# Routed-expert stage of a two-layer decoder step: gather in float32r parts, packed token slots, turned router product, extra-item table beside item 0

## The chip, the cores and the metric

The kernel runs on one core of a Trainium2 chip, as one program. The metric is the device time of an execution in microseconds (us). A core has five engines with instruction streams of their own: PE (TensorE, the 128x128 matrix array; its weight loads are shown apart as PEld), DVE (VectorE), ACT (ScalarE), POOL (GpSimd) and SP (SyncE, which only issues DMA here). They wait for each other through semaphores. SBUF is the on-chip memory of 128 partitions; PSUM has eight banks of 128 x 512 fp32, into which PE writes. TensorE's clock is granted at one of two levels, 2.4 GHz (1.00 in the profile) and 1.2 GHz (0.50).

## The reference

One inference step of two layers over 288 tokens (256 of a prompt, 8 x 4 of samples), 1024 features. Each layer has a mixer of four head groups with a projection, a residual and a LayerNorm, then a feed-forward part, again with residual and LayerNorm. Layer 0's feed-forward part is a dense SwiGLU. Layer 1's is the one that the change touches:

```python
logits = (h @ w_router).astype(jnp.float32)          # 8 experts
top_logit, top_e = lax.top_k(logits, TOP_K)          # the best two for each token
gates = jax.nn.softmax(top_logit, axis=-1)
...
def expert_block(args):                              # a block of up to 128 tokens of one expert
    tok, e = args
    xb = h_pad[tok]
    return (jax.nn.silu(xb @ w_gate[e]) * (xb @ w_up[e])) @ w_down[e]
...
f = zeros.at[sorted_tok].add(y_assign * w_assign[:, None])
h = layer_norm(ALPHA * h + f, ln_ffn_g, ln_ffn_b)
```

The hidden width is 3584. All values are fp32, and the result must be that of fp32 products.

## The kernel before

Everything is laid out with features in partitions: `h` and `r` are 8 blocks (KB) of 128 features x 288 tokens. The two layers run one after the other. All weights come as a stream of 1 MB chunks (128 x 2048 fp32) through a ring of six slots (`ring`), in the order in which they are used; SP issues the load of a chunk when the chunk six places earlier has been cut (`lo_done`).

*Cutting.* A product of fp32 values is made as three products of the type float32r (fp32r), which is of less precision: each operand is split into a high part, rounded to fp32r by an ACT copy, and a low part, which DVE gets by subtracting the high part. hi x hi, hi x lo and lo x hi are summed in PSUM. So each weight chunk costs ACT one copy (`w_hi`, L883 in the expert part) and DVE one subtraction (`w_lo`, L1253). `w_hi` and `w_lo` have three places each (SPLIT), and a chunk can be cut when PE is done with the chunk three places earlier (`chunk_done`).

*Routing* (ahead of the experts). When the LayerNorm `mix1` has given all eight blocks of h, PE multiplies them by `w_router` (L581): weights are the tokens of h, moving are the 8 columns of the router, 3 tiles of tokens (128, 128, 32) x 8 blocks, in plain fp32. Then it transposes h into token rows (L589, 24 transposes); DVE and ACT copy these from PSUM to `h_tok`. DVE meanwhile finds the best two experts for each token in small steps, each of which waits for the one before it (`step`, semaphore `route`). PE counts the tokens of each expert in order (L596, L599), DVE makes of it each token's slot in each expert (`item_pos`) and its gate (`item_gate`), and `select` makes the 0/1 matrix `sel` of the first expert (tokens x 128 slots). Then follows the table of extra items: an expert with more than 128 tokens needs further items, and a list of them is worked out in some thirty small steps on 128 partitions (L1189 to L1216). It ends in `table`, whose first entry is the number of items; with these inputs it is 8, one for each expert. PE, ACT and DVE read it (`value_load`) before their loop over the items. Last come eight multiplications `r = ALPHA * h` (L1219).

*An item* is one expert with up to 128 token slots. PE gathers its tokens in two halves of four blocks (`gather`, L608): in each block the three token tiles of `h_tok` are the weights and `sel` is moving, 12 fp32 products of 128 columns for each half, into bank 2 or 3. ACT and DVE cut the result to `x_hi` and `x_lo`, columns 0 to 127 of each block of 288. Then PE does, in seven groups of 512 hidden columns, the gate and the up products (24 fp32r products of 512 columns each, L617, with x as weights and the weight chunk moving), a transpose of the activated values (L647) and the down products (24 as well, with `ad_hi` and `ad_lo` as weights). There are 42 chunks for each item (CPI). ACT does silu and the cuts, DVE the multiplication with up, the low parts and the cuts. The gather of the next item's first half stands behind the last transpose, ahead of the last down products, and that of its second half behind them; then PE spreads the item's output back to the tokens with the transposed `sel` (`scat`): 8 blocks of two products (L701, L702), each added to `r` by DVE (L1275, semaphore `added`). The output parts `y_hi` and `y_lo` lie in columns 128 to 255 of x_hi's and x_lo's blocks; DVE makes y_lo at L1267. The last item gathers once more, for nobody.

*The end.* When all additions are done, PE sums `r` for the last LayerNorm (`ffn1`; L410 the mean, L415 the squares), DVE and ACT finish it, and SP stores h in two halves.

The order on each engine is that of the program text; no scheduler changes it. The engine functions share only semaphores, so a step that is moved on one engine moves past the waits that stand there.

## Time and profile before

| | |
|---|---|
| time, median of 3 runs | 1707.34 us (1707.08 to 1708.59) |
| span of the profiled execution | 1707.8 us |
| PE / PEld / DVE / ACT / POOL busy | 94% / 81% / 73% / 57% / 8% |
| DMA | 428.63 MB, mean 251 GB/s |
| expert part, from the first gather to the end | 613.8 to 1707.8 us |

The page cuts the span in 40 slices. PE is at 9 tenths in nearly all of the expert part, and the granted clock is full there but for the first slice or so (PEclk). A matmul's duration in the trace is longer than the distance to the next one, since they are pipelined: what one costs is the distance of starts. One fp32 product is two records of the trace (and two weight loads), one fp32r product is one record. A wait that is put down to a semaphore names the instruction that came last.

### The profile page before, as it was taken

To read this page: it belongs to the slowest core of one execution; us is meant where nothing else is said; L and a number is where in the kernel's file an instruction comes from. 1 tells how busy PE (TensorE), PEld (TensorE's weight loads), DVE (VectorE), ACT (ScalarE), POOL (GpSimd) and SP (SyncE) were. 2 spreads that over 40 slices of the span, in tenths; PEclk is the share of its full clock that TensorE was granted. 3 is DMA by queue.
4 is the path that set the end of the run, shared out by engine and by line. 5 is a ranking of instruction groups with operands and counts; after the bars stand their busy time and mean duration, and the time that the engine had idled before them with its cause. 6 is when DMAs were issued, how large, how long until landed. Compare 5 with 4: busy or idle time off the path is not lost.

```text
span 1707.8 us, 22408 instructions
## 1 busy us (share of the span) xinstructions
PE 1604.5 (94%) x8460; PEld 1380.0 (81%) x8460; DVE 1245.5 (73%) x1176; ACT 966.8 (57%) x816; POOL 140.0 (8%) x128
## 2 busy tenths in 40 slices
PE   4868999989886799999999999999999999999996
PEld 3857999989785788888888888888888888888885
DVE  3894443444679458878878878888888888887883
ACT  4333333334433327767767767767767767776772
POOL 3545000000055200000000000000000000000000
PEclk8979999999998969999999999999999999999998
DMA  9328355445333609989988998998997997997980
GB/s 282 129 94 115 107 172 173 150 147 173 124 99 99 89 27 355 359 293 348 359 325 316 359 345 304 362 333 305 361 360 277 361 376 264 369 367 262 371 300 28
DMA packets 213985, 428.63 MB, mean 251 GB/s; under 512 B 9136, under 2 KB 66416, under 8 KB 213936
## 3 DMA queue, kind: packets, MB, share of 16 engines
q1 hardware_dynamic: 209024, 424.67, 70.1%
q0 software_dynamic: 1984, 2.10, 2.1%
q10 hardware_dynamic: 2928, 1.18, 0.3%
q8 instruction: 33, 0.54, 0.1%
q14 instruction: 16, 0.13, 0.0%
HBM read 425.55 MB, written 2.37 MB: 251 GB/s over the span
## 4 chain that ended last, share of the span: by engine, by line
issue 66%; PE 24%; DVE 7%; ACT 1%; DMA 1%; POOL 0%; SPq 0%; ACTq 0%; DVEq 0%; POOLq 0%
PE bank L437 21%; DVE work L1014 4%; DVE w_lo L917 2%; DMA ring<-in_w_in 1%; PE bank L410 1%; ACT h L806 0%; ACT w_hi L744 0%; PE bank L415 0%; PE bank L503 0%; PE bank L424 0%; DVE r L910 0%; POOL rstd_tok L1289 0%; DVE r L944 0%; DVE work L1010 0%; DVE h L944 0%
## 5 line engine op out<-in xcount | busy, mean ns | idle before, releaser
L1253 DVE TENSOR_TENSOR w_lo<-ring,w_hi 128x2048 fp32r<-128x2048 f32 x320 | 732.3, 2290 | 120.0 <-ACT w_hi L883 119.1
L883 ACT ACTIVATE w_hi<-ring 128x2048 fp32r<-128x2048 f32 x320 | 614.1, 1919 | 181.3 <-PE bank L617 181.2
L617 PE MATMUL bank<-w_hi,x_hi 128*128 128x512 f32 x896 | 360.4, 402 | 0.3
L617 PE MATMUL bank<-w_hi,x_lo 128*128 128x512 f32 x896 | 354.1, 395 | 0.0
L617 PE MATMUL bank<-w_lo,x_hi 128*128 128x512 f32 x896 | 353.3, 394 | 0.0
L437 PE MATMUL bank<-x_hi,w_hi 128*128 128x288 f32 x832 | 255.1, 307 | 13.2 <-DVE x_lo L923 10.7
L437 PE MATMUL bank<-x_lo,w_hi 128*128 128x288 f32 x832 | 250.8, 301 | 0.0
L437 PE MATMUL bank<-x_hi,w_lo 128*128 128x288 f32 x832 | 249.8, 300 | 0.0
L617 PEld LDWEIGHTS bank<-w_hi,x_lo 128*128 128x128 f32 x896 | 168.8, 188 | 40.0
L617 PEld LDWEIGHTS bank<-w_hi,x_hi 128*128 128x128 f32 x896 | 169.0, 189 | 38.2 <-issue 2.1
L617 PEld LDWEIGHTS bank<-w_lo,x_hi 128*128 128x128 f32 x896 | 169.6, 189 | 37.0
L744 ACT ACTIVATE w_hi<-ring 128x2048 fp32r<-128x2048 f32 x68 | 129.4, 1908 | 108.6 <-PE bank L437 106.4
L617 PE MATMUL bank<-w_hi,ad_hi 128*128 128x512 f32 x448 | 175.7, 392 | 0.0
L917 DVE TENSOR_TENSOR w_lo<-ring,w_hi 128x2048 fp32r<-128x2048 f32 x60 | 139.8, 2330 | 48.6 <-ACT w_hi L744 48.3
L617 PE MATMUL bank<-w_lo,ad_hi 128*128 128x512 f32 x448 | 175.0, 391 | 0.0
L617 PE MATMUL bank<-w_hi,ad_lo 128*128 128x512 f32 x448 | 174.4, 389 | 0.0
L437 PEld LDWEIGHTS bank<-x_hi,w_hi 128*128 128x128 f32 x832 | 161.7, 194 | 15.0 <-issue 10.9
L437 PEld LDWEIGHTS bank<-x_lo,w_hi 128*128 128x128 f32 x832 | 161.8, 194 | 0.6
L437 PEld LDWEIGHTS bank<-x_hi,w_lo 128*128 128x128 f32 x832 | 161.9, 195 | 0.0
L1289 POOL TENSOR_TENSOR rstd_tok<-var_tok,minus_half 128x3 f32<-128x3 f32 x9 | 9.2, 1020 | 1490.2 <-DVE var_tok L936 1490.2
L617 PEld LDWEIGHTS bank<-w_hi,ad_hi 128*128 128x128 f32 x448 | 84.1, 188 | 19.3
L617 PEld LDWEIGHTS bank<-w_hi,ad_lo 128*128 128x128 f32 x448 | 84.1, 188 | 18.0
(194 smaller groups left out, 1670.8 us busy)
## 6 DMA issues: line engine op xcount, KB each, us to landing
ring<-in_w_e_gate SPq DMA_DIRECT2D x112, 1024.0 KB, 5.6
ring<-in_w_e_up SPq DMA_DIRECT2D x112, 1024.0 KB, 5.4
ring<-in_w_e_down SPq DMA_DIRECT2D x112, 1024.0 KB, 5.5
ring<-in_w_in SPq DMA_DIRECT2D x16, 1024.0 KB, 9.2
ring<-in_w_ff_gate SPq DMA_DIRECT2D x14, 1024.0 KB, 5.0
ring<-in_w_ff_up SPq DMA_DIRECT2D x14, 1024.0 KB, 5.1
ring<-in_w_ff_down SPq DMA_DIRECT2D x14, 1024.0 KB, 4.9
ring<-in_w_out SPq DMA_DIRECT2D x8, 1024.0 KB, 5.5
```

The costliest lines, as they stand in the source:

```text
L410: last = mm(bank[6][:, 0:TOKENS], weights[:, :], x[:, b, :], start=(b == 0), stop=(b == nb - 1))
L437: ins = mm(out, w, x, start=(first and n == 0), stop=(last and n == 2), skip_group_check=True)
L617: ins = mm(out, x, w[slot][:, columns], start=(first and n == 0), stop=(last and n == 2), skip_group_check=True)
L744: A(w_hi[c % SPLIT][:, :], ring[c % SLOTS][:, :], ACT.Copy).then_inc(hi_done, 1)
L883: A(w_hi[(START + p) % SPLIT][:, :], ring[(START + p) % SLOTS][:, :], ACT.Copy).then_inc(hi_done, 1)
L917: V.tensor_tensor(w_lo[c % SPLIT][:, :], ring[c % SLOTS][:, :], w_hi[c % SPLIT][:, :].bitcast(F32), ALU.subtract).then_inc(lo_done, 1)
L1014: V.scalar_tensor_tensor(out=out, in0=src, scalar=w, in1=out, op0=ALU.mult, op1=ALU.add).then_inc(conv_a, 1)
L1253: V.tensor_tensor(w_lo[(START + p) % SPLIT][:, :], ring[(START + p) % SLOTS][:, :], w_hi[(START + p) % SPLIT][:, :].bitcast(F32), ALU.subt ...
L1289: G.tensor_tensor(rstd_tok[:, :], var_tok[:, :], minus_half[:, :], ALU.pow).then_inc(ln_rs, 1)
```

## The change

Five edits:

1. The gather is made of fp32r products. `h_tok` becomes `h_tok_hi` and `h_tok_lo` (ACT copies, DVE subtracts, six pieces each in the order TURNS), `sel` is fp32r itself (0 and 1 are exact), and each of the 12 fp32 products becomes two fp32r products. All token tiles are taken with 128 rows; POOL writes zeros in the third tile first (`pad_ready`).
2. The token slots lie packed: `xs_hi`, `xs_lo`, `y_hi` and `y_lo` are views of x_hi and x_lo with 128 columns for each block, one behind the other, where they were columns of blocks of 288.
3. The router's logits come in the other orientation: the 8 columns of w_router are the weights and h moves (288 columns), one product for each block of h as soon as it is there, followed by the two transposes of this block's full token tiles. DVE copies the 8 x 288 logits (`logit_t`), and PE transposes them (three small transposes). The logits wait no more for st_v and for all of ln_out.
4. The table of extra items and `r = ALPHA * h` leave the way to item 0. They are a generator (`extra_items`), of which DVE runs two steps behind each cut of item 0. The number of items is therefore read only ahead of item 7: PE and ACT loop over items 0 to 6 and then from 7, DVE has item 0 written out, then 1 to 6, then from 7. In items up to 6 the cuts for the next item need no condition.
5. The last LayerNorm sums into bank 0 in place of 6 and waits for each block's addition by itself; the output is stored in four pieces in place of two.

```diff
-        h_tok, at = part(work, at, TT, D_MODEL)
         gate_e, at = part(work, at, 2, GC)
-        sel, at = part(work, at, TT, W)
         sel_w, at = part(work, at, TT, W)
+
+        def over_work(name, shape):
+
+            nonlocal at
+            t = nc.alloc_sbuf_tensor_at(name, shape, F32R, offset=work_at + 4 * at)
+            at += int(np.prod(shape[1:]))
+            assert at <= FB * TOKENS
+            return t
+
+        h_tok_hi = over_work("h_tok_hi", [P, TT, D_MODEL])
+        h_tok_lo = over_work("h_tok_lo", [P, TT, D_MODEL])
+        sel = over_work("sel", [P, TT, W])
         at = 0
 
-        y_hi, y_lo = x_hi[:, :, W:2 * W], x_lo[:, :, W:2 * W]
+        def slots_of(x, n):
+            flat = x[:, :, :].rearrange("p k t -> p (k t)")
+            return flat[:, n * KB * W:(n + 1) * KB * W].rearrange("p (k n) -> p k n", k=KB)
+
+        xs_hi, xs_lo = slots_of(x_hi, 0), slots_of(x_lo, 0)
...
+        y_hi, y_lo = slots_of(x_hi, 1), slots_of(x_lo, 1)
...
+        MEAN_BANK = {n: 0 if n == "ffn1" else 6 for n in LNS}
+        TURNS = [(0, 0), (1, 0), (0, 1), (1, 1), (2, 0), (2, 1)]
...
+            for q in range(4):
+                sp.wait_ge(ln_out, LN_AT["ffn1"] + 2 * (q + 1))
+                sp.dma_start(y_out[:, 2 * q:2 * q + 2, :], h[:, 2 * q:2 * q + 2, :]).then_inc(st_y, 16)
+            sp.wait_ge(st_y, 64)
...
-            pe.wait_ge(ln_out, LN_AT["mix1"] + KB)
+            def turn_tokens(t, k):
+                rows = TILE_ROWS[t]
+                return nc.tensor.transpose(bank[2 + 2 * t + k // 4][0:rows, k % 4 * P:(k % 4 + 1) * P],
+                                           h[:, k, t * P:t * P + rows], ident)
+
+            for k in range(KB):
+                pe.wait_ge(ln_out, LN_AT["mix1"] + k + 1)
+                last = mm(bank[0][0:N_EXPERTS, 0:TOKENS], w_router[:, k, :], h[:, k, :], start=(k == 0),
+                          stop=(k == KB - 1))
+                if k == KB - 1:
+                    last.then_inc(logits_ready, 1)
+                for t in range(2):
+                    last = turn_tokens(t, k)
+                    if k % 4 == 3:
+                        last.then_inc(h_turned, 1)
+            for half in range(2):
+                for k in range(4 * half, 4 * half + 4):
+                    last = turn_tokens(2, k)
+                last.then_inc(h_turned, 1)
+            pe.wait_ge(logits_out, 1)
             for t in range(TT):
                 rows = TILE_ROWS[t]
-                for k in range(KB):
-                    last = mm(bank[0][0:rows, t * 8:t * 8 + 8], h[:, k, t * P:t * P + rows], w_router[:, k, :],
-                              start=(k == 0), stop=(k == KB - 1))
-            last.then_inc(logits_ready, 1)
-
-            for t in range(TT):
-                rows = TILE_ROWS[t]
-                for half in range(2):
-                    for k in range(4):
-                        last = nc.tensor.transpose(bank[2 + 2 * t + half][0:rows, k * P:(k + 1) * P],
-                                                   h[:, 4 * half + k, t * P:t * P + rows], ident)
-                    last.then_inc(h_turned, 1)
+                last = nc.tensor.transpose(bank[1][0:rows, 64 + t * 8:64 + t * 8 + 8], logit_t[0:8, t * P:t * P + rows],
+                                           ident[0:8, 0:8])
+            last.then_inc(logits_turned, 1)
...
-                        rows = TILE_ROWS[t]
-                        last = mm(bank[2 + half][:, k % 4 * W:(k % 4 + 1) * W],
-                                  h_tok[0:rows, t, k * P:(k + 1) * P], sel[0:rows, t, :],
-                                  start=(t == 0), stop=(t == TT - 1))
+                        for rows in (h_tok_hi, h_tok_lo):
+                            last = mm(bank[2 + half][:, k % 4 * W:(k % 4 + 1) * W],
+                                      rows[:, t, k * P:(k + 1) * P], sel[:, t, :],
+                                      start=(t == 0 and rows is h_tok_hi), stop=(t == TT - 1 and rows is h_tok_lo))
...
+            pe.wait_ge(pad_ready, 3)
+            pe.wait_ge(h_tok_lo_done, 6)
             gather(0, 0)
             gather(0, 1)
             pe.sem_inc(chunk_done, SPLIT)
-            pe.wait_ge(table_ready, 1)
-            n_items = pe.value_load(table[0:1, 0:1], min_val=N_EXPERTS, max_val=N_EXPERTS + MAX_EXTRA)
-            with pe.Fori(0, n_items) as i:
+            pe.sem_inc(added, KB)
+
+            def item(i):
...
-            pe.wait_ge(added, n_items * KB + KB)
-            large_ln("ffn1", lambda b: None)
+
+            with pe.Fori(0, N_EXPERTS - 1) as i:
+                item(i)
+            pe.wait_ge(table_ready, 1)
+            n_items = pe.value_load(table[0:1, 0:1], min_val=N_EXPERTS, max_val=N_EXPERTS + MAX_EXTRA)
+            with pe.Fori(N_EXPERTS - 1, n_items) as i:
+                item(i)
+            large_ln("ffn1", lambda b: pe.wait_ge(added, n_items * KB + b + 1))
...
-            for t in range(TT):
+            for n, (t, half) in enumerate(TURNS):
                 rows = TILE_ROWS[t]
-                act.wait_ge(h_turned, 2 * t + 2)
-                A(h_tok[0:rows, t, 512:1024], bank[3 + 2 * t][0:rows, :], ACT.Copy).then_inc(h_tok_act, 1)
+                if n == 4:
+                    act.wait_ge(pad_ready, 3)
+                act.wait_ge(h_turned, n + 1)
+                A(h_tok_hi[0:rows, t, half * 512:(half + 1) * 512], bank[2 + 2 * t + half][0:rows, :],
+                  ACT.Copy).then_inc(h_tok_hi_done, 1)
...
-            dve.wait_ge(ln_out, LN_AT["mix1"] + KB)
-            dve.wait_ge(st_v, 128)
             step(V.memset(logit[:, :, :], 0.0))
             dve.wait_ge(logits_ready, 1)
-            V.tensor_copy(logit[:, 0:2, :], bank[0][:, 0:16].rearrange("p (t e) -> p t e", t=2))
-            V.tensor_copy(logit[0:N_SAMPLE, 2, :], bank[0][0:N_SAMPLE, 16:24]).then_inc(route, 1)
+            V.tensor_copy(logit_t[0:N_EXPERTS, :], bank[0][0:N_EXPERTS, 0:TOKENS]).then_inc(logits_out, 1)
+            dve.wait_ge(logits_turned, 1)
+            V.tensor_copy(logit[:, 0:2, :], bank[1][:, 64:80].rearrange("p (t e) -> p t e", t=2))
+            V.tensor_copy(logit[0:N_SAMPLE, 2, :], bank[1][0:N_SAMPLE, 80:88]).then_inc(route, 1)
...
-            for t in range(TT):
-                dve.wait_ge(h_turned, 2 * t + 1)
-                rows = TILE_ROWS[t]
-                V.tensor_copy(h_tok[0:rows, t, 0:512], bank[2 + 2 * t][0:rows, :]).then_inc(h_tok_dve, 1)
+            dve.wait_ge(pad_ready, 3)
+            for n, (t, half) in enumerate(TURNS):
+                dve.wait_ge(h_tok_hi_done, n + 1)
+                rows, at = TILE_ROWS[t], slice(half * 512, (half + 1) * 512)
+                V.tensor_tensor(h_tok_lo[0:rows, t, at], bank[2 + 2 * t + half][0:rows, :],
+                                h_tok_hi[0:rows, t, at].bitcast(F32), ALU.subtract).then_inc(h_tok_lo_done, 1)
...
+            def extra_items():
+
+                for d in range(KB):
+                    V.tensor_scalar(r[:, d, :], h[:, d, :], ALPHA, None, ALU.mult).then_inc(r_start, 1)
+                    yield
...
+                        next(beside, None)
...
+            beside = extra_items()
+            item(0, beside=beside)
+            for _ in beside:
+                pass
+            with dve.Fori(1, N_EXPERTS - 1) as i:
+                item(i)
+            dve.wait_ge(table_ready, 1)
+            n_items = dve.value_load(table[0:1, 0:1], min_val=N_EXPERTS, max_val=N_EXPERTS + MAX_EXTRA)
+            with dve.Fori(N_EXPERTS - 1, n_items) as i:
+                item(i, n_items)
...
+                if layer + 1 == DEPTH:
+                    pool.wait_ge(st_v, 64 * DEPTH)
+                    pool.wait_ge(ln_xn, LN_AT["mix1"] + KB)
+                    for v in (h_tok_hi, h_tok_lo, sel):
+                        G.memset(v[:, 2, :].bitcast(F32), 0.0).then_inc(pad_ready, 1)
```

On PE, between the LayerNorm mix1 and the first item. Before (L581 router, L589 transposes of h with the identity in `cst`, L596 and L599 counts, L608 the two gathers of item 0, all of `work`, where h_tok and sel lie):

```order
L424 MATMUL bank<-cst,rstd_tok 128x32
L581 MATMUL bank<-w_router,h 128x8 x16
L581 MATMUL bank<-w_router,h 32x8 x8
L589 MATMUL bank<-cst,h 128x128 x16
L589 MATMUL bank<-cst,h 32x128 x8
L596 MATMUL bank<-ybuf,cst 128x8
...
L599 MATMUL bank<-ybuf,ones 128x8 x3
L608 MATMUL bank<-work 128x128 x24
L627 TENSOR_LOAD table
```

and now (L607 router, L602 transposes of h, L622 transposes of the logits, L641 gather):

```order
L447 MATMUL bank<-cst,rstd_tok 128x32
L607 MATMUL bank<-h,w_router 8x288
L602 MATMUL bank<-cst,h 128x128 x2
...
L602 MATMUL bank<-cst,h 32x128 x8
L622 MATMUL bank<-cst,ybuf 128x8 x2
L622 MATMUL bank<-cst,ybuf 32x8
L629 MATMUL bank<-ybuf,cst 128x8
...
L641 MATMUL bank<-sel,h_tok_hi 128x128
L641 MATMUL bank<-sel,h_tok_lo 128x128
```

The router's products and the transposes take turns, block by block (eight such pairs), ahead of the third tile's transposes; the read of the table has left this place, and a gather has 24 products in place of 12.

On DVE, from the first selection to the cuts of item 0. Before (L1171 the selection, L1186 the counts, L1189 to L1216 the table, L1219 r, L1225 x_lo of item 0, L1234 sel_w, L1253 the first cut):

```order
L1171 TENSOR_SCALAR work<-cst,ybuf 32x128
...
L1186 COPY ybuf<-bank 128x8
L1189 TENSOR_SCALAR ybuf<-ybuf 128x8
...
L1216 CAST table<-ybuf 1x5
L1219 TENSOR_SCALAR r<-h 128x288 x8
L1225 TENSOR_TENSOR x_lo<-bank,x_hi 128x4x128 x2
L1230 TENSOR_LOAD table
...
L1253 TENSOR_TENSOR w_lo<-ring,w_hi 128x2048
```

and now (L1230 the selection, L1245 the counts, L1297 x_lo, L1306 sel_w, L1325 the cuts, L1250 r, L1254 and on the table, L1315 the multiplication with up):

```order
L1230 TENSOR_SCALAR sel<-cst,ybuf 32x128
...
L1245 COPY ybuf<-bank 128x8
L1297 TENSOR_TENSOR x_lo<-bank,x_hi 128x512 x2
...
L1325 TENSOR_TENSOR w_lo<-ring,w_hi 128x2048
L1250 TENSOR_SCALAR r<-h 128x288 x2
...
L1315 TENSOR_TENSOR work<-work,bank 128x512
L1325 TENSOR_TENSOR w_lo<-ring,w_hi 128x2048
L1254 TENSOR_SCALAR ybuf<-ybuf 128x8
```

The table's 29 instructions and the eight of r stand behind the first 17 cuts of item 0 now, where they stood ahead of x_lo.

## Rows read from the trace of the kernel before

The rows stand in groups, in the order in which the prediction comes to them. In rows of parts 5 of the page and of the groups of instructions the columns are: line, engine, operation, output<-inputs, shapes, count, then busy us and mean ns of one, then the idle time ahead of them and what ended it.

**Rows 1.** Part 1 of the page: busy us, share of the span, instructions.

```profile
PE 1604.5 (94%) x8460; PEld 1380.0 (81%) x8460; DVE 1245.5 (73%) x1176; ACT 966.8 (57%) x816; POOL 140.0 (8%) x128
```

**Rows 2.** Busy time by stage, one item: us, each engine's, clock, DMA, GB/s.

```profile
760.45:892.30 131.85, 131.72 (x607) 107.40 (x607) 110.81 (x74) 92.36 (x65) 0.00 (x0) 1.00 0.92 334
```

**Rows 3.** Parts 5 and 6 of the page: DVE's cuts; the weight loads.

```profile
L1253 DVE TENSOR_TENSOR w_lo<-ring,w_hi 128x2048 fp32r<-128x2048 f32 x320 | 732.3, 2290 | 120.0 <-ACT w_hi L883 119.1
...
ring<-in_w_e_down SPq DMA_DIRECT2D x112, 1024.0 KB, 5.5
```

**Rows 4.** Waits of SyncE's queue: us in total, times, longest.

```profile
SPq L382 <- DVE w_lo L1253: 815.9, 314, 55.0
```

**Rows 5.** Timeline, item 0 to item 1: start us, us, engine, line, operation, count.

```profile
746.64 4.19 PE L608 MATMUL bank<-work 128*128 128x128 f32 x24
...
750.76 0.19 PEld L617 LDWEIGHTS bank<-w_hi,ad_hi 128*128 128x128 f32 x1
750.87 0.19 PEld L617 LDWEIGHTS bank<-w_lo,ad_hi 128*128 128x128 f32 x1
751.10 0.39 PE L617 MATMUL bank<-w_lo,ad_hi 128*128 128x512 f32 x1
751.33 0.40 PE L617 MATMUL bank<-w_hi,ad_lo 128*128 128x512 f32 x1
...
756.34 4.18 PE L608 MATMUL bank<-work 128*128 128x128 f32 x24
757.98 1.40 DVE L1267 SCALAR_TENSOR_TENSOR x_lo<-bank,ybuf,x_hi 128x512 fp32r<-128x512 f32 x2
760.45 0.40 PE L701 MATMUL bank<-scat,x_hi 128*128 128x288 f32 x1
```

**Rows 6.** Timeline of PE in narrow windows: in the gather; one-column fp32 products.

```profile
746.98 0.69 PE L608 MATMUL bank<-work 128*128 128x128 f32 x3
...
747.18 0.79 PE L608 MATMUL bank<-work 32*128 32x128 f32 x3
...
769.12 0.38 PE L675 MATMUL bank<-ones,work 128*128 128x1 f32 x2
...
769.12 0.49 PE L675 MATMUL bank<-ones,work 128*128 128x1 f32 x3
```

**Rows 7.** Timeline, start of the expert part.

```profile
592.89 4.25 ACT L806 ACTIVATE h<-r,vec 128x288 f32<-128x288 f32 x8 [4.88 <-DVE r L944]
597.19 7.95 PE L581 MATMUL bank<-w_router,h 128*128 128x8 f32 x48 [4.83 <-ACT h L806]
...
605.07 5.38 PE L589 MATMUL bank<-cst,h 128*128 128x128 f32 x24
...
612.62 0.18 DVE L1163 SCALAR_TENSOR_TENSOR ybuf<-bank,ybuf 128x24 f32<-128x24 f32 x1 [2.23 <-issue]
...
621.60 1.82 DVE L1219 TENSOR_SCALAR r<-h 128x288 f32<-128x288 f32 x8
```

**Rows 8.** Busy time by stage, start of the expert part.

```profile
597.00:605.00 8.00, 7.81 (x48) 7.79 (x48) 0.08 (x1) 0.14 (x1) 0.00 (x0) 0.50 0.00 0
613.80:628.60 14.80, 14.74 (x48) 11.20 (x48) 9.09 (x44) 0.60 (x1) 0.00 (x0) 0.51 0.00 0
628.60:634.50 5.90, 5.90 (x15) 4.62 (x15) 3.08 (x5) 4.15 (x4) 0.00 (x0) 0.50 0.00 0
```

**Rows 9.** Groups of instructions: DVE on a 128x512 piece.

```profile
L1225 DVE TENSOR_TENSOR x_lo<-bank,x_hi 128x512 fp32r<-128x512 f32 x18 | 12.4, 691 | 44.3 <-ACT x_hi L857 44.3
```

**Rows 10.** One line, L617: duration ns min/median/max.

```profile
L617 PE MATMUL bank<-w_hi,x_lo x896: 387/396/628, 629.6 to 1661.6; 128*128 128x512 f32 x180
...
L617 PE MATMUL bank<-w_hi,ad_lo x448: 387/389/398, 656.0 to 1677.2; 128*128 128x512 f32 x150
```

**Rows 11.** Timeline of PE at the last LayerNorm.

```profile
1685.95 5.78 PE L410 MATMUL bank<-r,ones_model 128*128 128x288 f32 x16 [2.00 <-DVE r L1275]
```

**Rows 12.** Busy time by stage, the same stretch.

```profile
1685.90:1689.30 3.40, 3.35 (x7) 2.50 (x8) 0.00 (x0) 0.00 (x0) 0.00 (x0) 0.50 0.00 0
```

134 lines of the change are left out of this document (78 added, 56 removed).

## The prediction

> **What bounds the kernel now.** I read the page first, then the busy time by stage, the end of an item and the start of the next one instruction by instruction, and last the start of the expert part and the end of the kernel. The page says PE 94% busy, DVE 73%, ACT 57% [rows 1]; the chain of waits names no cause within the expert part, so it is of no use there. The stage table is: one item lasts 131.85 us, in which PE is busy for 131.72, DVE for 110.8 and ACT for 92.4 [rows 2]. TensorE bounds an item, and what it need not do comes off the time as long as nobody else gets late. The transfers do not yet: they land 5.5 us after their issue [rows 3], and SyncE spends 815.9 us waiting until DVE frees a slot of the ring [rows 4]. Around the last products of an item stand two gathers: from 746.64 to 750.76 (4.12 us) and from 756.34 to 760.45 (4.11 us) [rows 5]. Each is 12 fp32 products, which the trace shows as 24 records. So 8.23 us of each 131.85 are gathers.
>
> **The price of a gather, before.** The first four records, of two full tiles, start 0.113 us apart (746.64 to 746.98); then the 32-row tile begins 0.20 later [rows 5, 6]. Six records at 0.11 would be 0.67 us, while a group of three products takes 4.12/4 = 1.03: a third of the gather is the change of row size. After the change all three tiles have 128 rows, so this part goes. The Trainium skill (TensorEngine Tiling, Key Properties) says that a change of tiling mode drains the engine; the trace agrees, with about 0.09 us at that change. The rule speaks against the new router, which goes from 128 to 8 weight columns and back for each block.
>
> **The price of a gather, after.** It has 24 fp32r products with 128 moving columns. No row shows that shape. fp32r products with 512 columns start 0.23 us apart (751.10, 751.33) [rows 5]; in proportion 128 columns would take 0.057, the low end. But each product needs new weights. The first two fp32r loads after a gather are 0.11 apart (750.76, 750.87) [rows 5], and fp32 products with a single moving column take 0.11 more for one more [rows 6]: a load of 128 columns costs 0.11 whatever streams. The high end: fp32r gains nothing when few columns stream, and costs what the fp32 product of this very shape costs, two records, 0.22. I take 0.11, since the loads show it. A gather is then 24 x 0.11 = 2.64 us, the two 5.28 instead of 8.23: 2.95 less for each item. Eight items (the last one gathers too): -23.6. By the low end a gather is 1.37, another 20 off; by the high end 5.28, which is 1.17 more than now, and 16 of them +18.7 in place of -23.6.
> The Trainium skill (TensorE: Matmul & The Clock Gate, LDWEIGHTS) gives 128/1.2 = 107 ns for such a load, and the 0.11 confirms it. The same page (Weight-path perf modes) has a fast weight load for 128 columns of any type but FP32; by that rule fp32r would be near the low end. The two loads 0.11 apart do not show it.
>
> **Does anyone get late in an item?** After the second stretch of products the scatter needs y_lo, which DVE makes from 757.98 to 759.38, while the scatter starts at 760.45 [rows 5]. The first gather's end, and with it all of this, comes 1.48 earlier: y_lo from 756.5, its first half at 757.2, its second at 757.9. The scatter wants to start at 760.45 - 2.95 = 757.5; its first four blocks need the first half only. It just fits. DVE has 110.8 us of work in an item of then 128.9, so it stays below PE. Six chunks of 12 products at 0.23 take PE 16.6 us, three times the 5.5 of a landing, so the ring of six slots holds.
>
> **The start of the expert part.** ACT writes the eight h from 592.89 to 597.14; only then does the router start and take 7.95 us, and 24 transposes 5.38; DVE goes on with the counts at 612.62 and begins r at 621.60 [rows 7]. The gathers fill 613.8 to 628.6; the clock is half (1.2 GHz) then, in the router and until 634.5 [rows 8].
> - The router and the transposes now start with the first h, at 593.5. Eight router products of 288 columns are 16 records like those of L410: 5.78 us with 3.4 of them at half clock, so 4.1 at full [rows 11, 12] and 8.2 at half. With 24 transposes at 0.22 and 16 changes of columns at 0.09 that is 14.9 at half clock, 7.5 at full. If the clock rises some 6 us after the work starts, as it did in item 0 (628.6 to 634.5 [rows 8]), 60% are left for full clock: 4.5 more, so 604, and the three transposes of the logits 0.5 later, against 605.1 for the logits before: -0.6. Bounds: -3 at full clock, +4 at half.
> - DVE now has six subtractions of 0.69, as L1225 [rows 9], where it had three copies: at least three pieces more, +2. But before it stood idle for 2.23 us ahead of 612.62 [rows 7], because PE's counting stood behind the transposes; that wait goes. Both together: nothing. The first selection comes 0.6 earlier.
> - The 48 gather products: 0.22 each at half clock for 6 us (27 of them), then 21 at 0.11: 8.3 us against 14.8, -6.5 (-4.3 if the clock stays low). And item 0 starts at full clock: 5.9 us of half clock become 2.95: -3.
> - Sum of the start: -10 (from -4 to -13).
> - The table of extra items is 29 of the 41 small steps between 612.62 and 621.60, 0.22 each, so 6.4 us, and r 1.82 us [rows 7]: all of it lay beside the gathers. Now it stands between the cuts of item 0, two steps behind each of 17 cuts: 8.2 us more for DVE. Six chunks take PE 16.6 and four transposes, about 17.1; DVE needs 6 x 2.29 [rows 3] and two pieces of 0.69, 15.1, and with 12 steps 17.8 to 18. One microsecond late a group over three groups, less a lead of about one and a half: +1.5 (0 to 5).
> - The table is long ready when item 7 reads it. The read and the further copies of the loop I cost at nothing, since only one item boundary has them and PE is fed ahead there; +1 if not.
>
> **The end.** PE waited 2.00 us for the last addition, and L410 then ran at a clock of 0.50 for 3.4 us: 5.78 us, to 1691.73 [rows 11, 12]. Now each block's sum follows its addition, in a bank that the scatter does not use at that moment. From 1683.95 at full clock it ends at 1688.0: -3.7 (-2 if the clock drops all the same). The last output piece is half as big, 0.3 MB less at some 334 GB/s [rows 2]: -0.8. Sum -4.5.
>
> **Packing.** Gate and up products, whose weights are x_hi and x_lo at a step of 288, have a median of 396 ns; down products, whose weights lie packed at 128, 389 [rows 10]. If the step were the cause, the packed slots would give up to 6 ns x 2688 products = 16 us. The two kinds also differ in the banks they write and in how often they change them, and no row tells these apart. I put packing at nothing, and keep the 16 for the range.
>
> **The sum.** -23.6 - 10 + 1.5 - 4.5 = -36.6 from the span of the profiled execution, 1707.8, is 1671.2. The page gives no time around the span; the median of the runs, 1707.34, lies 0.5 below it. So 1670.7, rounded to 1670.
>
> **Rivals.**
> - Slower: fp32r with 128 moving columns takes as long as fp32 does. Its place is every gather, its price 24 x 0.22 = 5.28 against 4.11, +18.7 over 16 gathers; of the start's gain -4 is left, the end stays at -4.5, item 0 at +1.5: 1707.8 + 11.7, less 0.5, is 1719. A gather gets slower from 0.171 a product on (4.11/24), the kernel from about 0.19. For it: this kernel uses fp32r with 288 columns or more alone. Against it: the loads.
> - The change doesn't do what it says: the code turns fp32r of this width into the two records of fp32. The time is the same 1719.
> - Packing works (-16): 1655. For it the two medians, against it nothing but the other differences.
> - The low end, loads hidden (-20): 1651.
> - The boundary gives back half: once the gathers shrink, y_lo, x_lo and the additions on DVE are the chain, and PE waits 1.5 us an item, +12: 1682. For it: the margin above is 0.3 us. Against: DVE has 18 us an item to spare.
>
> **Chances and range.** Forecast 0.51 (1664 to 1676), half given back 0.11, packing 0.13, low end 0.05, fp32's price for fp32r 0.18 (both ways to it), gains and losses that cancel 0.02. 1650 to 1696 holds the first four and leaves the rest out. A measurement can tell 0.2%, 3.4 us, from no change: faster 0.80, same 0.02, slower 0.18.
>
> **What would show it.** In the gather 24 records, 0.11 apart at full clock and without a gap of 0.2; an item of 128.9 us; the first sum of the last norm beginning before the last addition ends; in item 0 a DVE without idle and PE waiting 1 to 2 us for w_lo. I am wrong if the fp32r records stand 0.2 apart, if gate and up products drop to 389 ns, or if PE waits for y_lo ahead of the scatter.

## The result, and the profile after

The kernel after takes 1662.66 us (median of 4 runs, 1661.68 to 1666.74), the kernel before 1707.62 us (4 runs, 1707.08 to 1708.59). The ratio is 0.9739 with a 95% interval of 0.9728 to 0.9751: faster by 45 us, where 1670 us in a range from 1650 to 1696 was forecast. The time lies inside the range, but below the band from 1664 to 1676 to which the forecast gave its chance of 0.51.

The profiled execution of after is its slowest run, 1666.74 us with a span of 1665.0. Both kernels run the same code up to the last LayerNorm ahead of the router, yet its first sum starts at 584.77 us here and at 580.44 in before. In the other kernels of this study it starts between 580.7 and 587.3, so the stretch ahead of it differs by up to 6.8 us from one execution to the next. It is left out of every comparison below; times are measured from that first sum on. From it to the end of the span before takes 1127.4 us and after 1080.2, 47.1 less.

Part 1 of the page, after, against [rows 1] (busy us, share of the span, instructions):

```profile
PE 1563.0 (94%) x8431; PEld 1362.1 (82%) x8431; DVE 1246.0 (75%) x1180; ACT 964.7 (58%) x817; POOL 141.8 (9%) x131
```

PE has 41.5 us less, DVE and ACT what they had: nobody else's work shrank, and TensorE still bounds the kernel. Next the boundary of items 0 and 1 in the timeline of after, against [rows 5] (start us, us, engine, line, operation, count), with records of the second gather picked out:

```profile
751.31 0.22 PE L641 MATMUL bank<-sel,h_tok_hi 128*128 128x128 f32 x1
751.37 0.28 PE L641 MATMUL bank<-sel,h_tok_lo 128*128 128x128 f32 x1
751.48 0.27 PE L641 MATMUL bank<-sel,h_tok_hi 128*128 128x128 f32 x1
751.59 0.28 PE L641 MATMUL bank<-sel,h_tok_lo 128*128 128x128 f32 x1
751.71 0.28 PE L641 MATMUL bank<-sel,h_tok_hi 128*128 128x128 f32 x1
...
752.95 1.41 DVE L1344 SCALAR_TENSOR_TENSOR x_lo<-bank,ybuf,x_hi 128x512 fp32r<-128x512 f32 x2
753.94 0.35 PE L735 MATMUL bank<-scat,x_hi 128*128 128x288 f32 x1
```

The 24 records stand 0.11 apart (0.06 between the first two) and without the gap of 0.2 at the change of row size. The gather takes 753.94 - 751.31 = 2.63 us (2.71 for the other one), where it took 4.11. y_lo, the low part of the item's output (L1344), begins 0.99 ahead of the scatter and its first half is done when the scatter starts: it just fits. The stage table of one whole item, after, against [rows 2]:

```profile
753.94:880.90 126.96, 126.90 (x607) 106.05 (x607) 110.76 (x75) 92.23 (x64) 0.00 (x0) 1.00 0.95 347
```

An item went from 131.6 (mean of the seven steps from scatter to scatter, 760.45 to 1681.55) to 127.06, so by 4.5 where the gathers explain 2.9. The rest is in the gate and up products. One line, L650, after, against [rows 10] (duration ns min/median/max):

```profile
L650 PE MATMUL bank<-w_hi,x_lo x896: 387/389/628, 627.4 to 1626.5; 128*128 128x512 f32 x180
```

Their median is 389 now, where it was 396; the down products had 389 all along. Last the end of the kernel, after, against [rows 11]:

```profile
1644.78 3.00 DVE L1353 TENSOR_TENSOR r<-r,bank 128x288 f32<-128x288 f32 x8
...
1645.65 4.09 PE L432 MATMUL bank<-r,ones_model 128*128 128x288 f32 x16
...
1659.28 3.48 SPq L419 DMA_DIRECT2D out_y_t<-h  x4
```

The mean sums start while DVE is still adding (L1353 ends at 1647.78), wait for nothing and take 4.09 us at full clock instead of 5.78.

All of it together, in us, from the two profiled executions:

| stretch | before | after | difference |
|---|---|---|---|
| up to the last norm ahead of the router (same code) | 580.44 | 584.77 | +4.3 |
| from there to the first gather product | 33.42 | 31.42 | -2.0 |
| the 48 gather products of item 0 | 14.76 | 10.27 | -4.5 |
| first product of item 0 to its scatter | 131.83 | 127.48 | -4.3 |
| first to eighth scatter (7 items) | 921.10 | 889.40 | -31.7 |
| eighth scatter to the end | 26.24 | 21.65 | -4.6 |

### The profile page after: what moved, and what is told of

It is laid out like the page before. It is cut to its first block, busy times and chain, and to the rows that moved or that the text cites. A ratio compares the mean times of both kernels' runs of the same rounds, so it can differ in the third digit from the quotient of the medians.

```text
span 1665.0 us, 22278 instructions
## 1 busy us (share of the span) xinstructions
PE 1563.0 (94%) x8431; PEld 1362.1 (82%) x8431; DVE 1246.0 (75%) x1180; ACT 964.7 (58%) x817; POOL 141.8 (9%) x131
## 4 chain that ended last, share of the span: by engine, by line
issue 65%; PE 23%; DVE 7%; DMA 3%; POOL 1%; ACT 1%; SPq 0%; ACTq 0%; POOLq 0%; DVEq 0%
PE bank L460 21%; DVE work L1071 4%; DVE w_lo L974 2%; DMA out_conv_c_s<-ext_c 1%; DMA ring<-in_w_in 1%; PE bank L432 1%; DVE r L1001 1%; PE bank L438 0%; PE bank L447 0%; PE bank L526 0%; POOL rstd_tok L1378 0%; ACT w_hi L784 0%; ACT h L846 0%; DVE r L966 0%; POOL ext_a L1396 0%
## 5 line engine op out<-in xcount | busy, mean ns | idle before, releaser
L1325 DVE TENSOR_TENSOR w_lo<-ring,w_hi 128x2048 fp32r<-128x2048 f32 x320 | 731.9, 2290 | 101.7 <-ACT w_hi L925 100.7
L650 PE MATMUL bank<-w_hi,x_hi 128*128 128x512 f32 x896 | 356.1, 397 | 1.4 <-issue 0.9
L650 PE MATMUL bank<-w_hi,x_lo 128*128 128x512 f32 x896 | 349.9, 390 | 0.0
L650 PE MATMUL bank<-w_lo,x_hi 128*128 128x512 f32 x896 | 349.2, 390 | 0.0
L650 PEld LDWEIGHTS bank<-w_hi,x_hi 128*128 128x128 f32 x896 | 168.7, 188 | 36.9 <-issue 2.7
L650 PEld LDWEIGHTS bank<-w_hi,x_lo 128*128 128x128 f32 x896 | 168.5, 188 | 36.1
L650 PEld LDWEIGHTS bank<-w_lo,x_hi 128*128 128x128 f32 x896 | 168.9, 188 | 33.0
L650 PE MATMUL bank<-w_hi,ad_hi 128*128 128x512 f32 x448 | 175.0, 391 | 0.1
L650 PE MATMUL bank<-w_hi,ad_lo 128*128 128x512 f32 x448 | 174.4, 389 | 0.0
L650 PE MATMUL bank<-w_lo,ad_hi 128*128 128x512 f32 x448 | 174.3, 389 | 0.0
L1378 POOL TENSOR_TENSOR rstd_tok<-var_tok,minus_half 128x3 f32<-128x3 f32 x9 | 9.2, 1024 | 1439.4 <-DVE var_tok L993 1439.4
L650 PEld LDWEIGHTS bank<-w_hi,ad_hi 128*128 128x128 f32 x448 | 84.1, 188 | 18.0 <-DVE w_lo L1325 0.6
L650 PEld LDWEIGHTS bank<-w_hi,ad_lo 128*128 128x128 f32 x448 | 84.1, 188 | 17.6
```

The source lines that it names most:

```text
L650: ins = mm(out, x, w[slot][:, columns], start=(first and n == 0), stop=(last and n == 2), skip_group_check=True)
L1325: V.tensor_tensor(w_lo[(START + p) % SPLIT][:, :], ring[(START + p) % SLOTS][:, :], w_hi[(START + p) % SPLIT][:, :].bitcast(F32), ALU.subt ...
L1378: G.tensor_tensor(rstd_tok[:, :], var_tok[:, :], minus_half[:, :], ALU.pow).then_inc(ln_rs, 1)
```

## Experiments

The kernel before was measured again beside each group; on those chips its median was 1710.0 to 1711.3, so kernels of different groups are compared by their ratio to it. "Item" is the mean step from scatter to scatter. The diffs show the main lines of each edit.

**Packing alone.** Before, with this one edit:

```diff
-        y_hi, y_lo = x_hi[:, :, W:2 * W], x_lo[:, :, W:2 * W]
+        xs_hi, xs_lo = slots_of(x_hi, 0), slots_of(x_lo, 0)
+        y_hi, y_lo = slots_of(x_hi, 1), slots_of(x_lo, 1)
```

> The kernel before with nothing changed but the slots of x and y, which lie packed 128 columns apart instead of in halves of rows 288 apart; gathers, router, table and the end stay as they were. Theory (the layout of the x slots is what made the gate and up products of an item slower than the down products): the spacing of the x products falls from about 232 ns to about 227, an item gets some 1.7 us shorter, and the kernel some 13 us: about 1694. Rival (the layout does nothing, and the 1.7 us an item come from something else in the change, such as the order of DVE's work or the shorter boundary): an item stays at 131.6 and the kernel at 1707.

Measured: 1696.95 us against 1711.15, ratio 0.9920 (0.9898 to 0.9942). An item takes 129.89 us instead of 131.59. One line of that kernel:

```profile
L622 PE MATMUL bank<-w_hi,x_lo x896: 386/390/629, 632.8 to 1650.6; 128*128 128x512 f32 x180
```

The theory holds: 1.7 us an item, some 14 us in all, from where the slots lie; nothing else was changed.

**All but packing.** After, with the slots back in halves of rows that are 288 columns apart (the edit above, reversed).

> The kernel after with the slots of x and y put back to halves of rows 288 apart, all else as after. Theory (the layout makes the gate and up products slower): an item lasts 128.6 instead of 126.9, the x products are about 232 ns apart again, and the time is about 1676. Rival (something else in the change made these products faster): 126.9 an item and 1663.

Measured: 1680.05 us, ratio 0.9819 (0.9796 to 0.9842), an item 128.75, and the products are slow again:

```profile
L646 PE MATMUL bank<-w_hi,x_lo x896: 387/396/628, 627.3 to 1639.1; 128*128 128x512 f32 x180
```

The same 1.7 us an item from the other side (1.0 in item 0, which takes 128.48 here and 127.48 in after). By the ratios packing is worth 8.0 thousandths in both comparisons, about 14 us.

**Distance or address of the slots.** Two versions of after that differ in the step between slots alone:

First 256 columns, x and y side by side:

```diff
-            return flat[:, n * KB * W:(n + 1) * KB * W].rearrange("p (k n) -> p k n", k=KB)
+            return flat[:, 0:2 * KB * W].rearrange("p (k n) -> p k n", k=KB)[:, :, n * W:(n + 1) * W]
```

> The kernel after with the slots of x and y 256 columns apart (1024 bytes) in place of 128 (512 bytes). Theory (the address of a slot within some power of two counts: slots on multiples of 512 bytes are loaded without loss): the x products stay at 227 ns, an item at 126.9, the time at 1663. Rival (the distance between the slots counts, and 128 columns is the only one without a gap): the x products go to 230 ns or more, an item to 128 or more, the time to 1672 or more.

Then 144 columns:

```diff
-            return flat[:, n * KB * W:(n + 1) * KB * W].rearrange("p (k n) -> p k n", k=KB)
+            return flat[:, n * KB * 144:(n + 1) * KB * 144].rearrange("p (k n) -> p k n", k=KB)[:, :, 0:W]
```

> The kernel after with the slots of x and y 144 columns apart (576 bytes), so close together but not on multiples of 512 bytes. Theory (the address counts): the x products go back to about 232 ns, an item to 128.6, the time to 1676. Rival (the distance counts, short ones are fine): 227 to 228 ns, 127.0 an item, 1663 to 1665.

Measured: at 256 columns 1666.28 us, ratio 0.9739 (0.9720 to 0.9758), an item 127.06: the same as packed. At 144 columns 1679.37, ratio 0.9817 (0.9798 to 0.9836), an item 128.67: as slow as 288. One line of each, first 256, then 144:

```profile
L650 PE MATMUL bank<-w_hi,x_lo x896: 388/389/629, 627.0 to 1626.0; 128*128 128x512 f32 x180
```

```profile
L650 PE MATMUL bank<-w_hi,x_lo x896: 388/392/628, 629.3 to 1640.6; 128*128 128x512 f32 x180
```

Closeness does not help, and distance does not hurt. Steps of 512 and 1024 bytes are fast, steps of 576 and 1152 bytes slow. The gate and up products (x products, for short) of the items start 229.5 ns apart on average at the first two steps, 233.7 at 576 bytes and 234.2 at 1152. What separates the four is that the step is a multiple of 512 bytes, or is not. Multiples of 128 bytes do not suffice, since 1152 is nine of them; multiples of 256 were not tried.

Whether each slot's own address counts, or the step between them, these runs cannot tell, and the trace speaks against the simple reading. At a step of 1152 bytes the fifth slot starts at 4608, a multiple of 512 from the tile's start like the slots of after. Yet its three products stand 233.2, 232.9 and 228.5 ns behind the ones ahead of them in the run with all but packing, and 226.6 to 226.7 in after. The products that follow are slowed as well: the second to eighth of each 24 down products, whose weights lie packed in every kernel, stand 230.0 ns apart there and 227.1 in after, and from the ninth on 226.7 in both. A run with a step of 512 bytes and a start that is not a multiple of it would separate the two, and was not made. Nor can this say which unit is slowed down: the records of the weight loads have a median of 188 ns in all of them.

**Padding alone.** Before, still with an fp32 gather, but with the third token tile filled up to 128 rows with zeros:

```diff
-                                  h_tok[0:rows, t, k * P:(k + 1) * P], sel[0:rows, t, :],
+                                  h_tok[:, t, k * P:(k + 1) * P], sel[:, t, :],
```

> The kernel before with one change: the third token tile of the gather has 128 rows, filled up with zeros, and the gather stays in fp32. Theory (a third of the gather was the change of row size; the split into a high and a low part gives nothing by itself, since an fp32 product is two records of the same length anyway): a gather falls from 4.12 us to 24 x 0.112 = 2.7, an item by 2.8 us, the kernel by about 24 us, to 1684. Rival (the fp32r form is what made the gather shorter): a gather keeps 4.1 us or falls by no more than 0.5 us, and the kernel stays within 4 us of 1707.

Measured: 1682.88 us against 1711.15, ratio 0.9838 (0.9822 to 0.9855), an item 128.71. Its two gathers at the first boundary:

```profile
744.78 2.84 PE L609 MATMUL bank<-work 128*128 128x128 f32 x24
752.96 2.84 PE L609 MATMUL bank<-work 128*128 128x128 f32 x24
755.55 0.38 PE L703 MATMUL bank<-scat,x_hi 128*128 128x288 f32 x1
```

From 752.96 to 755.55 are 2.59 us, even less than the 2.63 of after. The whole gain of the gather comes from the padding. The product of a high and a low part, which gives the change its name, gives nothing.

The time fell by 28.3 us where 24 were expected, and item 0 shows a part of the rest: it takes 126.14 us up to its scatter instead of 131.83, and two gathers explain only 3.0 of these 5.7. The clock was half for 5.9 us of item 0 in before. Here it is back at full 5.8 us after the first gather product, ahead of item 0.

Padding alone and packing alone make 0.0162 and 0.0080 of the ratio, together 0.0242 of the 0.0261 of the whole change. If the two add up, which was not run, the fp32r products, the router, the table and the end bring 3 us between them, and that is within the intervals.

**The other half of that cross.** After, with fp32r products and the third tile in its 32 rows:

```diff
-                                      rows[:, t, k * P:(k + 1) * P], sel[:, t, :],
+                                      rows[0:n_rows, t, k * P:(k + 1) * P], sel[0:n_rows, t, :],
```

> The kernel after with the third token tile of the gather in its 32 rows again, so that the row size changes; the products stay fp32r with a high and a low part. Theory (the change of row size is what costs): a gather goes from 2.67 us back to about 4.1, as before the change; an item becomes 2.9 us longer, the kernel about 24 us: 1686. Rival (fp32r products do not pay for a change of row size, or pay less, and their form is the gain): a gather stays below 3 us, an item at 127 to 127.5 and the kernel below 1668.

Measured: 1695.95 us (1689.89 to 1711.67 in 10 runs), ratio 0.9923 (0.9895 to 0.9952). The undisturbed gathers take 3.72 to 3.87 us, a little under the 4.1 expected and far above the rival's 3. The time is 10 us above the 1686 that was expected. The profiled execution took 1710.23 us, 14 more than the median, so what follows need not have this size in the others. Its items take 130.5 to 134.4, which nobody had expected. The stage table around the boundary of two items, cut where the clock changes (the last three numbers are clock, DMA share and GB/s):

```profile
873.00:879.90 6.90, 6.90 (x41) 5.76 (x40) 5.00 (x3) 2.52 (x2) 0.00 (x0) 0.98 1.00 335
879.90:886.70 6.80, 6.80 (x18) 5.37 (x18) 2.98 (x2) 3.12 (x3) 0.00 (x0) 0.52 0.71 255
886.70:892.50 5.80, 5.80 (x35) 4.88 (x33) 3.61 (x3) 2.46 (x3) 0.00 (x0) 1.00 0.66 213
892.50:893.80 1.30, 1.30 (x9) 1.24 (x8) 0.50 (x1) 1.11 (x2) 0.00 (x0) 0.82 1.04 400
893.80:896.60 2.80, 2.80 (x12) 2.71 (x12) 2.80 (x9) 2.68 (x2) 0.00 (x0) 0.50 0.28 109
```

The first gather of this boundary ends at 880.46. From 879.9 on the granted clock is 0.50, the lower of its two levels, for 7 us, and once more in the scatter, although PE's records show it busy throughout. In this execution it falls at each of the eight boundaries. The fp32 gather with the very same change of rows never loses the clock in an item, in before and in the packing run. The padded fp32r gathers of after never lose it in an item either. So it is the two together, fp32r and the row changes, that lose it; that was seen, not explained.

**One fp32 copy.** After, with the padding kept, one fp32 product instead of two, and no subtractions:

```diff
-                        for rows in (h_tok_hi, h_tok_lo):
-                            last = mm(bank[2 + half][:, k % 4 * W:(k % 4 + 1) * W],
-                                      rows[:, t, k * P:(k + 1) * P], sel[:, t, :],
-                                      start=(t == 0 and rows is h_tok_hi), stop=(t == TT - 1 and rows is h_tok_lo))
+                        last = mm(bank[2 + half][:, k % 4 * W:(k % 4 + 1) * W],
+                                  h_tok[:, t, k * P:(k + 1) * P], sel[:, t, :],
+                                  start=(t == 0), stop=(t == TT - 1))
```

> The kernel after with one copy of the tokens in fp32 in place of a high and a low part: one fp32 product where two fp32r ones stood, the third tile padded to 128 rows as before, and without the six subtractions of 0.6 us on DVE. Theory (padding the rows is the whole gain, and an fp32 product costs as much as two fp32r ones): a gather takes 2.6 us as in the kernel before with padded rows, an item 126.8, and the first gather starts up to 3 us earlier, since the subtractions stood ahead of the slot positions; the kernel takes 1659 to 1662. Rival (fp32r is needed for part of the gain, such as the clock or the spacing beside the down products): an item above 127.5, the kernel at 1668 or more.

Measured: 1661.85 us, ratio 0.9713 (0.9696 to 0.9730). An item is 127.13, 0.07 above after. The first gather product starts 30.68 us after the norm's first sum instead of 31.42, not up to 3 earlier: without the subtractions DVE is idle until PE's counts are there. The larger part was in no expectation: the 48 gather products of item 0 take 7.27 us instead of 10.27. First the stage table of after, then that of this kernel:

```profile
616.19:626.46 10.27, 10.27 (x48) 10.27 (x49) 1.71 (x7) 0.60 (x1) 0.00 (x0) 0.50 0.01 2
626.46:629.73 3.27, 3.27 (x9) 2.59 (x10) 1.45 (x4) 3.00 (x3) 0.00 (x0) 0.50 0.00 0
629.73:640.00 10.27, 10.27 (x49) 8.38 (x48) 8.11 (x10) 8.56 (x7) 0.00 (x0) 1.00 0.57 205
```

```profile
616.05:620.00 3.95, 3.95 (x18) 3.95 (x19) 1.03 (x6) 0.00 (x0) 0.00 (x0) 0.50 0.02 4
620.00:623.32 3.32, 3.32 (x32) 3.32 (x31) 0.69 (x1) 0.60 (x1) 0.00 (x0) 0.99 0.00 0
```

In both PE is busy without a gap. In the fp32 gather the clock is back at full after 4.0 us; in the fp32r gather it stays half to the last product and 3.3 us into the item. From the norm's first sum to the end this kernel takes 1075.7 us and after 1080.2: the split into two parts costs 4.5 us.

**The table ahead of item 0.** After, with the table and the start of r where before had them:

```diff
+            beside = extra_items()
+            for _ in beside:
+                pass
             tokens_lo(0, 0)
...
-            item(0, beside=beside)
+            item(0)
```

> The kernel after with the whole table of extra items and the start of r ahead of item 0 on DVE, where the kernel before has them. Theory (beside the cuts they cost PE about 2 us of waiting; ahead of item 0 they lie beside the first gathers, which now take 10.3 us, more than the 8.2 us of table and start of r): x_lo of item 0 is ready no more than 2 us later than now, PE does not wait for w_lo in item 0, and the kernel stays within 3 us of 1663. Rival (moving them beside the cuts is what made item 0 shorter): item 0 up to its scatter takes 4 us or more longer and the kernel 1667 or more.

Measured: 1666.17 us, ratio 0.9730 (0.9707 to 0.9753). The first gather product and the gathers stand as in after; the first product of item 0 comes right behind them, and from it to the scatter it takes 125.92 us instead of 127.48. The weight loads waited for w_lo in item 0 of after, and here no such line is left. Waits of the loads in item 0, after (us in total, times, longest):

```profile
PEld bank L650 <- DVE w_lo L1325: 1.8, 3, 0.6
```

The steps beside the cuts cost 1.6 us. With gathers of 10.3 us they had a place to hide ahead of item 0; the move was a loss of 1.6. In the ratio this is one thousandth, less than its interval.

**Both of these together.** The two edits above in one kernel.

> The kernel after with the tokens in one fp32 copy, the third tile padded (as in the run fp32_padded_b), and with the table of extra items and the start of r ahead of item 0 (as in the run table_ahead_b). Theory (the two savings are in different places and add up: the first gather 0.7 us earlier and no six subtractions, item 0 without the waits for w_lo that the small steps caused, 1.6 us): the kernel is 1.5 to 2 us below the kernel with fp32 alone, a ratio to the kernel before of 0.970 to 0.9705. Rival (with the table ahead of item 0, x_lo of item 0 comes later than the shorter gathers, and eats the 1.6 us): the same ratio as fp32 alone, 0.9713, or above.

Measured: 1666.19 us, ratio 0.9739 (0.9726 to 0.9753). The rival has it. The timeline at the start of item 0:

```profile
616.31 7.54 PE L639 MATMUL bank<-work 128*128 128x128 f32 x48 [1.34 <-DVE work L1223]
...
626.61 0.49 PE L648 MATMUL bank<-w_hi,x_hi 128*128 128x512 f32 x1 [2.75 <-DVE x_lo L1290]
```

The gathers end after 7.5 us, DVE is still in the table, and PE waits 2.75 us for x_lo. From 627.2 to 630.5 the clock is half again. From the norm's first sum to the end the traces give 1080.2 us for after, 1078.6 with the table ahead, 1075.7 with the fp32 copy, and 1078.6 with both. So the two savings do not add up: the table ahead of item 0 makes the fp32 kernel 2.9 us slower, because it had counted on gathers of 10.3 us to lie beside. By the ratios the kernel with both is no faster than after.

**One step a cut.** The fp32 kernel with one small step behind each cut in place of two:

```diff
                         next(beside, None)
-                        next(beside, None)
```

> The kernel after with the tokens in one fp32 copy, the third tile padded (as in the run fp32_padded_b), and one small step of the table behind each cut of item 0 in place of two; those left over run behind item 0's work. Theory (two steps a cut make DVE slower than PE's groups of six chunks for a while, one does not: 6 x 2.29 + 2 x 0.69 + 6 x 0.25 = 16.6 us against 17.1 of PE): item 0 up to its scatter 124.4 to 125.0 us instead of 126.1, the kernel 1 to 1.6 us below fp32 alone, a ratio to the kernel before of 0.9705. Rival (the small steps are not what item 0 loses; or the steps left over delay the start of item 1): no change, 0.9713, or more.

Measured: 1658.71 us (1657.88 to 1663.08), ratio 0.9713 (0.9694 to 0.9731). Item 0 up to its scatter takes 124.71 us, and of the waits one is left:

```profile
PEld bank L648 <- DVE w_lo L1318: 0.4, 1, 0.4
```

In item 0 the 1.4 us are there (124.71 against 126.08), as the theory has them. The profiled execution as a whole does not show them. From the first sum to the end it takes 1075.6 us against 1075.7, because its clock was half for 6.8 us from the router's start instead of 3.4, and for 5.0 us of the first gathers instead of 4.0: these start 0.78 later and take 0.45 more. In the ratio they are not to be seen either: its interval is 3.7 thousandths wide, the gain below one. The forecast of 0.9705 is neither met nor refuted.

**The old end.** After, with the sums of the last norm behind all additions:

```diff
-        MEAN_BANK = {n: 0 if n == "ffn1" else 6 for n in LNS}
+        MEAN_BANK = {n: 6 for n in LNS}
...
-            large_ln("ffn1", lambda b: pe.wait_ge(added, n_items * KB + b + 1))
+            large_ln("ffn1", lambda b: pe.wait_ge(added, n_items * KB + KB))
```

> The kernel after with the mean sums of the last norm in the scatter's bank again and after the last addition, as in the kernel before; the output stays in four pieces. Theory (the sums beside the additions are most of the gain at the end, and the half clock of the kernel before came from the wait): from the last scatter's start to the first sum 4.4 us instead of 2.3, and the sums at half clock for part of their time; the end grows by 2.1 to 3.7 us, the time from 1663 to about 1666. Rival (the output pieces and chance make up most of it): less than 1.5 us.

Measured: 1669.02 us (1665.86 to 1671.49), ratio 0.9752 (0.9737 to 0.9767). From the last scatter to the end it takes 23.89 us instead of 21.65, and the sums wait and then run at full clock:

```profile
1650.34 4.15 PE L432 MATMUL bank<-r,ones_model 128*128 128x288 f32 x16 [2.02 <-DVE r L1353]
```

So 2.2 us for the sums. Half of the theory failed: PE waited 2.02 us as in before, and the clock stayed full, so the wait by itself does not bring the half clock. In the runs with the old end, packing alone and padding alone, the end takes 24.61 and 24.79 us; 0.7 to 0.9 above this one, which is the output in four pieces. The 26.2 of before hold another 1.5 us of half clock that these two did not have.

**The old router.** After, with 24 products of 8 moving columns behind the last h, then the transposes:

```diff
-            for k in range(KB):
-                pe.wait_ge(ln_out, LN_AT["mix1"] + k + 1)
-                last = mm(bank[0][0:N_EXPERTS, 0:TOKENS], w_router[:, k, :], h[:, k, :], start=(k == 0),
-                          stop=(k == KB - 1))
...
+            pe.wait_ge(ln_out, LN_AT["mix1"] + KB)
+            for t in range(TT):
+                rows = TILE_ROWS[t]
+                for k in range(KB):
+                    last = mm(bank[0][0:rows, t * 8:t * 8 + 8], h[:, k, t * P:t * P + rows], w_router[:, k, :],
+                              start=(k == 0), stop=(k == KB - 1))
...
```

> The kernel after with the logits in the old orientation: 24 products with 8 moving columns once all eight blocks of h are there, then the transposes; no copy and no three transposes of the logits. Theory (the new orientation by itself is nearly worth nothing, because at half clock its 16 records of 288 columns and 16 changes of columns cost what the early start saves): from the last mean sum's start to the first gather 31.4 to 33 us instead of 31.4, the time within 1.5 us of 1663. Rival (the new router is what made the start shorter): 33.4 us or more, and 1665 or more.

Measured: 1669.46 us, ratio 0.9755 (0.9742 to 0.9769). 32.78 us to the first gather instead of 31.42, and item 0 up to its scatter 128.73 instead of 127.48, because the clock rises 15.5 us after the first gather product, not 13.5. The theory's range held the first number. But the time rose by 1.6 thousandths against after, 2.7 us, which is the rival's number for the time, though not for the start: 1.4 of it from the start itself, 1.2 from the clock behind it. The intervals of the two ratios overlap, so this rests on the traces, which differ by 2.8 us from the first sum to the end.

## Why the prediction was right, and where it was not

**The gathers: right.** 24 records at 0.11 were forecast from the two loads in [rows 5], 2.64 us a gather; 2.63 and 2.71 came. Eight items with two gathers saved 23 us (forecast 23.6). The step that took a third of the gather for the change of row size (0.67 us of 1.03 would be left) is what the padding run shows to be the whole gain. What the prediction did not draw from it: the 24 fp32 records of before were already 0.11 apart, so two records of fp32 and two products of fp32r cost the same, and the split was not needed. The rival that gave fp32r the price of fp32, 0.22 a product, is refuted by every gather of after. It was a rival built on the wrong comparison: in fp32 a product at this shape is two records of 0.11, and fp32r is one.

**Packing: the term that was mis-sized.** The prediction saw the two medians of [rows 10], worked out 16 us, and put packing at nothing, with a chance of 0.13, because the banks and their changes differ too. It is 1.7 us for each of eight items, 13.6 us, shown from both sides. That the banks differ was no evidence against it. The prediction had named as a sign of being wrong that the gate and up products drop to 389 ns, and they did: of its rivals, the one in which packing works came true. It put this at 1655 us, by 16 in place of 13.6. That the time is still only 7.3 us below 1670 is luck in part: without packing the changed stretches save 47.1 - 13.6 = 33.5 us, where 36.6 were forecast, and the stretch that no edit touches differs by several us between executions.

**The first gathers and the clock of item 0: too good by 3.7 us.** Forecast was a clock that rises some 6 us after the gathers begin, -6.5 us. It stayed half for all 48 products, which is the -4.3 that stood beside it as the bound; -4.5 came. For item 0 at full clock -3 was forecast. The clock was half for 3.3 us of it instead of 5.9, so -1.3. The step that failed is the early rise of the clock: the prediction took it from item 0 of before, whose products have 512 columns, for fp32r products of 128. With padded fp32 products in the same place the clock rose after 4.0 to 5.8 us, as assumed.

**The start: right in size, by luck in part.** -0.6 for the first selection was forecast, -2.0 read from the profiles. The 33.42 us of before hold 17.1 us of half clock up to the counts. The packing and padding runs, with the old router, have 13.7 there and take 32.2 us. Against these it is -0.8. In it are +0.7 for the six subtractions, which the prediction held for hidden. They stood in its sum at nothing because a DVE wait of 2.23 us was to go in exchange.

**The table beside item 0: right.** +1.5 forecast, +1.6 measured. The read of the table ahead of item 7 was put at 0, +1 if not: the last of the seven items takes 127.75 where the others take 126.94, +0.8.

**The end: right, but from a disturbed number.** -4.5 forecast, -4.6 read, -3.0 against executions without the half clock: 2.2 for the sums and 0.7 to 0.9 for the output, whose forecast was 0.8. The -3.7 for the sums held the 5.78 us of [rows 11], with 3.4 us at half clock, for a property of the kernel; the run with the old end has the same wait and 4.15 us.

**The boundary: right.** The rival in which the boundary gives back half of the gain did not come. y_lo starts 0.99 us ahead of the scatter, and PE does not wait for it.

By the trace, then: -23.1 for gathers, -13.6 for packing, -7.8 for the start with item 0's clock, +1.6 and +0.8 for the table, -4.6 for the end, +4.3 from code that did not change. That is -42.4 of the -42.8 between the spans. The forecast was -36.6.

## What to carry to other kernels

Before an operation is split into parts to make it cheaper, count the records it already is and look for the gap between them: here the gap was the row size, and zeros in the spare rows removed it. A difference of 2% in the median of two groups of otherwise equal instructions is worth an experiment of one line when there are 2688 of them. Two savings that fill the same idle time do not add up, so test them together too. And take a change of five edits apart: here two small ones, the zeros in the spare rows and the packed slots, make nearly all of the gain.

## What the runs showed of the hardware

- **How the stationary operands lie counts.** fp32r products with 512 moving columns, each with 128 weight columns, follow each other at 229.5 ns on average when these blocks of weights start 512 or 1024 bytes apart. At steps of 576 or 1152 bytes it is 233.7 and 234.2 ns.
- **One fp32 product costs about what two fp32r products cost, for 128x128 times 128 columns.** Two records at 0.108 us for one fp32 product (2.60 us for 24), two fp32r products at 0.11 (2.67 us for 24).
- **A change of row size costs 0.14 to 0.19 us at full clock.** In fp32 a gather of four blocks with two changes each takes 4.11 - 2.60 = 1.51 us more than without them, so 0.19 a change; in fp32r 3.8 - 2.67 = 1.1 us, so 0.14. Both take it that a 32-row product by itself costs what the others do, which was not measured. The prediction had read 0.09 from one pair of rows. The Trainium skill (TensorEngine Tiling (Array Packing), Key Properties) says that such a change drains the engine; these numbers agree, and are its price here.
- **The clock did not come back in the first fp32r gathers.** In the seven kernels with padded fp32r gathers it fell 1.5 to 3.7 us ahead of the gathers (in the counts) and rose 13.5 us (15.5 with the old router) after their start, which is 3.2 us (5.3) into the products with 512 columns. In the four kernels with padded fp32 gathers it rose 4.0 to 5.8 us after the start, still within them; in the two with 32-row fp32 tiles 19.4 and 20.7 us after it. PE was busy without a gap during these gathers in all of them. What in the form of the products makes the difference was not measured. The Trainium skill (TensorE: Matmul & The Clock Gate, What's actually happening) says that the gate goes by how busy PE has been. By the busy time in these records the kinds of gather cannot be told apart, so these numbers neither bear that out nor refute it.
